# Last output tile and final norm of a three-layer block in parts of 384 and 128 tokens, not two of 256

## The reference, cut to what matters

```python
def rmsnorm_2(x, w):
    xf = x.astype(jnp.float32)
    y = xf * lax.rsqrt(jnp.mean(xf * xf, axis=-1, keepdims=True) + EPS)
    return (y * w.astype(jnp.float32)).astype(x.dtype)
...
        h = rmsnorm_2(x, norm_ffn_w[l])
        x = x + (jax.nn.silu(h @ w_gate[l]) * (h @ w_up[l])) @ w_down[l]
    return rmsnorm_2(x, final_norm_w)
```

## Time and profile before

| | us |
|---|---|
| median of 3 runs (2475.85, 2475.42, 2472.47) | 2475.42 |
| profiled execution, own time | 2472.24 |
| profiled execution, span of the trace | 2470.5 |
| PE busy (98% of the span) | 2432.2 |
| DVE busy (64%) | 1586.6 |
| ACT busy (43%) | 1064.8 |
| POOL busy (29%) | 723.8 |

### The profile page before, as it was taken

How to read it: one execution, slowest core, us unless ns; L and a number is a source line. 1 busy time by engine, 2 the same in 40 slices (tenths; PEclk the granted TensorE clock), 3 DMA queues, 4 the chain that set the end, 5 groups by cost and what they waited for, 6 DMA issues and landing times.

```text
span 2470.5 us, 30455 instructions
## 1 busy us (share of the span) xinstructions
PE 2432.2 (98%) x11856; PEld 1991.7 (81%) x11856; DVE 1586.6 (64%) x2021; ACT 1064.8 (43%) x1695; POOL 723.8 (29%) x426
## 2 busy tenths in 40 slices
PE   8999999999999999999999999999999988999998
PEld 6888888778888888888887778888887866888887
DVE  7887427667888317887137667887326655888712
ACT  5555114564555215554005564555213565555500
POOL 1001666522000560002665531001564422100164
PEclk9999999999999999999999999999999999999999
DMA  4332222103222223232222112422223111233222
GB/s 181 118 120 77 86 94 77 60 35 120 105 101 103 86 94 128 91 131 69 94 94 69 54 51 102 161 95 93 86 94 137 52 44 32 106 120 120 77 86 77
DMA packets 52382, 229.42 MB, mean 93 GB/s; under 512 B 7184, under 2 KB 10128, under 8 KB 39056
## 3 DMA queue, kind: packets, MB, share of 16 engines
q1 hardware_dynamic: 50528, 225.66, 26.1%
q10 hardware_dynamic: 1712, 1.82, 0.2%
HBM read 225.36 MB, written 2.10 MB: 92 GB/s over the span
## 4 chain that ended last, share of the span: by engine, by line
PE 95%; DVE 2%; ACT 1%; issue 1%; POOL 0%; DMA 0%; ACTq 0%; SPq 0%; DVEq 0%; POOLq 0%
PE bank L816 13%; PE bank L817 13%; PE bank L818 13%; PE bank L941 13%; PE bank L940 13%; PE bank L939 13%; PE bank L961 2%; PE bank L1048 2%; PE bank L1033 2%; PE bank L888 1%; PE bank L889 1%; PE bank L890 1%; PE bank L1017 1%; PE bank L1018 1%; PE bank L833 1%; PE bank L1270 1%
## 5 line engine op out<-in xcount | busy, mean ns | idle before, releaser
L770 POOL TENSOR_SCALAR wh<-raw 128x1024 fp32r<-128x1024 f32 x192 | 210.1, 1094 | 1698.0 <-PE bank L941 1082.2
L773 POOL TENSOR_TENSOR wl<-raw,wh 128x1024 fp32r<-128x1024 f32 x192 | 469.4, 2445 | 16.0
L816 PE MATMUL bank<-act_all,wh 128*128 128x512 f32 (+1 forms) x902 | 353.8, 392 | 0.0
L818 PE MATMUL bank<-act_all,wl 128*128 128x512 f32 (+1 forms) x902 | 346.7, 384 | 0.0
L817 PE MATMUL bank<-act_all,wh 128*128 128x512 f32 (+1 forms) x902 | 346.3, 384 | 0.0
L2044 DVE SCALAR_TENSOR_TENSOR x<-bank,x 128x512 f32<-128x512 f32 x63 | 43.2, 690 | 412.4 <-PE bank L818 412.4
L939 PE MATMUL bank<-wh,ss 128*128 128x512 f32 x540 | 211.3, 391 | 2.3 <-DVE plast L2130 2.3
L940 PE MATMUL bank<-wh,ss 128*128 128x512 f32 x540 | 210.9, 390 | 0.0
L941 PE MATMUL bank<-wl,ss 128*128 128x512 f32 x540 | 210.7, 390 | 0.0
L1534 ACT ACTIVATE wh<-rawa 128x1024 fp32r<-128x1024 f32 x135 | 143.3, 1062 | 155.9 <-PE bank L941 153.6
L2107 DVE TENSOR_TENSOR wl<-rawa,wh 128x1024 fp32r<-128x1024 f32 x135 | 165.2, 1223 | 62.3 <-ACT wh L1534 62.2
(11 more groups left out here) (374 smaller groups left out, 5208.8 us busy)
## 6 DMA issues: line engine op xcount, KB each, us to landing
raw<-in_stream SPq DMA_DIRECT2D x192, 512.0 KB, 3.3
rawa<-in_gu SPq DMA_DIRECT2D x60, 1024.0 KB, 4.8
raw<-in_gu SPq DMA_DIRECT2D x40, 1024.0 KB, 4.8
raw<-in_gu_small SPq DMA_DIRECT2D x20, 512.0 KB, 3.3
x<-in_x SPq DMA_DIRECT2D x8, 256.0 KB, 6.3
w1k<-in_w1k SPq DMA_DIRECT2D x1, 2048.0 KB, 7.9
w1v_low<-in_w1v SPq DMA_DIRECT2D x1, 1024.0 KB, 5.6
w1v_high<-in_w1v SPq DMA_DIRECT2D x1, 1024.0 KB, 7.6
```

The lines of the kernel that those rows point to most:

```text
L770: nc.gpsimd.tensor_scalar(wh[:, h % 2, :, :], src, 1.0, 1.0, ALU.mult, ALU.mult)\
L773: nc.gpsimd.tensor_tensor(wl[:, h % 2, :, :], src, wh[:, h % 2, :, :].bitcast(F32), ALU.subtract).then_inc(split_done, 1)
L816: mm = nc.tensor.matmul(bank, wh[:, slot, k, :], rh, start=start, stop=False)
L818: return nc.tensor.matmul(bank, wl[:, slot, k, :], rh, start=False, stop=stop)
```

## The change

The two parts of the last tile and of the norm are tokens 0 to 383 and 384 to 511 (`LAST_CUT = 3` of four groups of 128). POOL scales three tiles, not two, so DVE scales five. The sums of squares of tiles 0 to 6 are no longer made in bank 0 and added by DVE: `partial_sums` leaves them in banks 1 and 5 with `stop=False`, and `last_sums` adds the last tile's to them there; ACT takes the root straight from PSUM with the mean's factor as scale and `EPS` (set once at the start in `fin_part`) as bias. The blocks' order is new. On DVE, three of the first part's five scalings (tiles 5, 6, 7) move behind the second part's update and inverse, and the writes are grouped anew.

```diff
-LAST_POOL = 2
+LAST_POOL = 3
+LAST_CUT = 3
+LAST_TILES = (range(0, LAST_CUT), range(LAST_CUT, NQ))
+LAST_COLUMNS = (slice(0, LAST_CUT * P), slice(LAST_CUT * P, T))
...
-            for half, m, count in ((0, LAST_POOL, 6), (0, 0, LAST_POOL), (1, 2, 2), (1, 4, 2), (1, 6, 2)):
-                c = slice(2 * P * half, 2 * P * half + 2 * P)
+            for half, m, count in ((0, LAST_POOL, 2), (0, 5, 3), (0, 0, LAST_POOL), (1, LAST_POOL, 3), (1, 6, 2)):
+                c = LAST_COLUMNS[half]
...
-                    sp.wait_ge(fin_done, 6 * half + m + count - LAST_POOL)
+                    sp.wait_ge(fin_done, (KT - LAST_POOL) * half + m + count - LAST_POOL)
...
             def partial_sums():
...
-                for i in range(NQ):
-                    mm = nc.tensor.matmul(B[0][:, i:i + 1], rstd[:, i * P:(i + 1) * P], ones[:, 0:1], start=True, stop=True)
-                mm.then_inc(part_sums, 1)
+                for half in range(2):
+                    for i in LAST_TILES[half]:
+                        nc.tensor.matmul(B[(1, 5)[half]][:, i:i + 1], rstd[:, i * P:(i + 1) * P], ones[:, 0:1],
+                                         start=(i == LAST_TILES[half][0]), stop=False, skip_group_check=True)
 
             def last_sums(half):
                 pe.wait_ge(half_sq, half + 1)
-                for i in range(2 * half, 2 * half + 2):
+                for i in LAST_TILES[half]:
                     mm = nc.tensor.matmul(B[(1, 5)[half]][:, i:i + 1], sq[:, 3, i * P:(i + 1) * P], ones[:, 0:1],
-                                          start=True, stop=True)
+                                          start=False, stop=True, skip_group_check=True)
...
             for f in range(6, 14):
                 last_block(f, 0)
-            for f in range(6, 9):
-                last_block(f, 1)
             partial_sums()
             for f in range(14, FT):
                 last_block(f, 0)
-            for f in range(9, 12):
+            for f in range(6, 13):
                 last_block(f, 1)
             last_sums(0)
-            for f in range(12, 15):
+            for f in range(13, 18):
                 last_block(f, 1)
             last_rows(0)
-            for f in range(15, FT):
+            for f in range(18, FT):
                 last_block(f, 1)
             last_sums(1)
             last_rows(1)
...
-                act.wait_ge(fin_step, 4 * half + 3)
-                nc.scalar.activation(fin4[:, 2 * half:2 * half + 2], fin4[:, 2 * half:2 * half + 2], ACT.Sqrt).then_inc(fin_root, 1)
+                act.wait_ge(fin_set, 2)
+                act.wait_ge(half_sums, half + 1)
+                nc.scalar.activation(fin4[:, w], B[(1, 5)[half]][:, w], ACT.Sqrt, bias=fin_part[:, 0:1], scale=1.0 / D)\
+                    .then_inc(fin_root, 1)
...
+            V.memset(fin_part[:, :], EPS).then_inc(fin_set, 1)
...
+            def last_update(half, bank):
+                c = LAST_COLUMNS[half]
+                V.scalar_tensor_tensor(x[:, KT - 1, c], bank[:, c], 1.0, x[:, KT - 1, c], ALU.mult, ALU.add)\
                     .then_inc(fin_step, 1)
...
+            def last_scale(half, tiles):
+                c = LAST_COLUMNS[half]
                 dve.wait_ge(fin_rows, 2 * half + 1)
-                for m in range(LAST_POOL, KT):
+                for m in tiles:
                     V.scalar_tensor_tensor(x[:, m, c], x[:, m, c], gains2[:, 3, m:m + 1], B[LAST_ROWS[half][0]][:, c],
                                            ALU.mult, ALU.mult).then_inc(fin_done, 1)
+
+            dve.wait_ge(half_done, 1)
+            last_update(0, B[7])
+            last_inverse(0)
+            last_scale(0, range(LAST_POOL, 5))
+            dve.wait_ge(*last_done(KT - 1))
+            last_update(1, B[3])
+            last_scale(0, range(5, 6))
+            last_inverse(1)
+            last_scale(0, range(6, KT))
+            last_scale(1, range(LAST_POOL, KT))
```

More of the change, by code:

```diff
@@ L484, in build @@
         half_sq = sem("half_sq")
-        part_sums = sem("part_sums")
         fin_step = sem("fin_step")
@@ L1409, in _ @@
             last = DOWN_AT[4]
-            halves = ((B[7], slice(0, 2 * P)), (B[3], slice(2 * P, T)))
+            halves = ((B[7], LAST_COLUMNS[0]), (B[3], LAST_COLUMNS[1]))
             def last_block(f, half):
@@ L1425, in partial_sums @@
                 pe.wait_ge(sq_used, 9 * 8 + KT + 3)
-                for i in range(NQ):
-                    mm = nc.tensor.matmul(B[0][:, i:i + 1], rstd[:, i * P:(i + 1) * P], ones[:, 0:1], start=True, stop=True)
-                mm.then_inc(part_sums, 1)
+                for half in range(2):
+                    for i in LAST_TILES[half]:
+                        nc.tensor.matmul(B[(1, 5)[half]][:, i:i + 1], rstd[:, i * P:(i + 1) * P], ones[:, 0:1],
+                                         start=(i == LAST_TILES[half][0]), stop=False, skip_group_check=True)
             def last_sums(half):
                 pe.wait_ge(half_sq, half + 1)
-                for i in range(2 * half, 2 * half + 2):
+                for i in LAST_TILES[half]:
                     mm = nc.tensor.matmul(B[(1, 5)[half]][:, i:i + 1], sq[:, 3, i * P:(i + 1) * P], ones[:, 0:1],
-                                          start=True, stop=True)
+                                          start=False, stop=True, skip_group_check=True)
                 mm.then_inc(half_sums, 1)
             def last_rows(half):
-                pe.wait_ge(fin_step, 4 * half + 5)
+                pe.wait_ge(fin_step, 3 * half + 3)
                 for bank in LAST_ROWS[half]:
-                    for i in range(2 * half, 2 * half + 2):
+                    for i in LAST_TILES[half]:
                         tr = nc.tensor.transpose(B[bank][:, i * P:(i + 1) * P], cos[:, i * P:(i + 1) * P], ident[:, :])
@@ L1948, in _ @@
             for half in range(2):
-                c = slice(2 * P * half, 2 * P * half + 2 * P)
-                act.wait_ge(fin_step, 4 * half + 2)
+                c = LAST_COLUMNS[half]
+                w = slice(LAST_TILES[half][0], LAST_TILES[half][-1] + 1)
+                act.wait_ge(fin_step, 3 * half + 1)
                 nc.scalar.activation(sq[:, 3, c], x[:, KT - 1, c], ACT.Square).then_inc(half_sq, 1)
-                act.wait_ge(fin_step, 4 * half + 3)
-                nc.scalar.activation(fin4[:, 2 * half:2 * half + 2], fin4[:, 2 * half:2 * half + 2], ACT.Sqrt).then_inc(fin_root, 1)
+                act.wait_ge(fin_set, 2)
+                act.wait_ge(half_sums, half + 1)
+                nc.scalar.activation(fin4[:, w], B[(1, 5)[half]][:, w], ACT.Sqrt, bias=fin_part[:, 0:1], scale=1.0 / D)\
+                    .then_inc(fin_root, 1)
                 act.wait_ge(fin_rows, 2 * half + 2)
@@ L1956, in _ @@
             act.wait_ge(fin_pool, 2 * LAST_POOL)
-            act.dma_start(d["out"][:, 0:LAST_POOL, 2 * P:T], x[:, 0:LAST_POOL, 2 * P:T]).then_inc(out_done, 16)
+            act.dma_start(d["out"][:, 0:LAST_POOL, LAST_COLUMNS[1]], x[:, 0:LAST_POOL, LAST_COLUMNS[1]]).then_inc(out_done, 16)
         @block.vector
@@ L2789, in _, with last_inverse @@
                     .then_inc(fin_step, 1)
[L2790 to L2793, removed]
+            def last_inverse(half):
+                c, tiles = LAST_COLUMNS[half], LAST_TILES[half]
+                w = slice(tiles[0], tiles[-1] + 1)
                 dve.wait_ge(fin_root, half + 1)
@@ L2795, in _ @@
                 V.reciprocal(fin4[:, w], fin4[:, w]).then_inc(fin_step, 1)
-                dve.wait_ge(fin_step, 4 * half + 4)
-                V.tensor_copy(cos[:, c].rearrange("p (c n) -> p c n", c=2),
-                              fin4[:, w].rearrange("p (c a) -> p c a", a=1).to_broadcast([P, 2, P])).then_inc(fin_step, 1)
+                dve.wait_ge(fin_step, 3 * half + 2)
+                V.tensor_copy(cos[:, c].rearrange("p (c n) -> p c n", c=len(tiles)),
+                              fin4[:, w].rearrange("p (c a) -> p c a", a=1).to_broadcast([P, len(tiles), P]))\
+                    .then_inc(fin_step, 1)
```

## The result

| | before | after |
|---|---|---|
| median, 19 runs each | 2474.15 | 2478.43 |
| lowest and highest | 2471.93, 2475.85 | 2475.83, 2480.23 |
| ratio, with its 95% interval | | 1.0018 (1.0011 to 1.0025) |
| profiled execution, own time | 2472.24 | 2479.03 |
| its span | 2470.5 | 2477.2 |

What follows compares the result with a forecast made beforehand. PE bounds until its last block, then the first late write's issue and the bytes behind it. Issue +2.0 us and 0.65 MB more +1.95 make +3.9 on 2475.42: 2479.3 us, range 2473.4 to 2481.3.

Steps and rivals of the forecast that it cites:

- What bounds the kernel: End of the last tile: PE until its last matmul, then the first late write's issue and the bytes still to write.
- Price of a matmul by width: PE's last tile: 0.173 us at 384 columns, 0.1115 at 128, probably a weight-load floor; last block 3.1 us later.
- Rival A: PE's narrow matmuls cost half of those of 256 columns: 3.0 us fall away, +0.9, 2476.3 us; chance 0.12.
- Covers: Last unit's split and first part's update, square and spread finish before PE asks for them; no wait added.
- The second part's chain: Update to rows after PE's last block: 2.25 us, 0.85 less than before.
- spread copy 0.23: DVE's copy spreading the second part's inverse over 128 columns was taken to last 0.23 us.
- inside DVE's time: POOL's scalings, first part 2463.9 to 2466.8, second 2467.3 to 2468.6, were to end within DVE's own time.
- DVE's order and the first late issue: On DVE, tiles 6 and 7 stand behind the spread; SP's first late issue at 2467.45, 2.0 us later.
- Writes: After the first late issue 1.70 MB are left, before 1.05; at 330 GB/s 5.15 us, 1.95 more.
- Rival B: The writes do not bind; 3.45 us follow the last issue: +1.9, 2477.3 us; chance 0.06.
- Rival C: Second part's 512-byte output runs cost DMA as much as 1024-byte ones: +5.5, 2480.9 us, deciding from 2.6; chance 0.16.
- Rival D: The shorter tail after PE's last block wins; a gain over the bound would need 5 us of 9.2; chance 0.04.

Runs made afterwards that it cites:

- Run 1: Kernel after, but POOL's three first-part tiles are written before DVE's fifth scaling is waited for; median 2476.55 us against 2472.84 before, ratio 1.0014.
- run 5: Also e5_early: kernel after, with DVE's five first-part scalings ahead of the second part's update, first part's sums and rows earlier on PE; 2474.59 us, ratio 1.0004 to before.
- Run 4: Kernel after, with the second part's matmuls computing 256 columns, 128 of them unread; one profile, 32.0 us from last tile's first matmul to end, against 31.5.
- Run 2: Kernel after, with POOL starting on the first part only after the second part's spread; one profile, still 31.5 us from last tile's first matmul to end.
- e6_best: Kernel after, cut at 256, POOL two tiles, first part scaled before second's update, second part's DVE writes in 1, 1, 2, 2 tiles; 2472.09 us, ratio 0.9995 to before.
- e7_single: As e6_best, but every tile of the second part is written by itself, POOL's too; 2472.21 us against 2472.39 before, ratio 1.0000.
- e3_cut2: Kernel after, with the cut back at 256 and 256 tokens, all else kept; 2473.72 us, ratio 1.0003 to before.

## Why the prediction was right, point by point

Two of the points below rest on rows of before that were not shown so far, of PE and of DVE and POOL:

```profile
1931.37 0.63 PE L1198 MATMUL bank<-w2v,hid 128*31 128x64 f32 x8
...
2414.22 0.68 DVE L2024 TENSOR_TENSOR rstd<-rstd,sq 128x512 f32<-128x512 f32 x1
...
2443.43 2.40 POOL L773 TENSOR_TENSOR wl<-raw,wh 128x1024 fp32r<-128x1024 f32 x1
2444.14 2.24 DVE L2024 TENSOR_TENSOR rstd<-rstd,sq 128x512 f32<-128x512 f32 x1
```

- **What bounds the kernel.** Right, PE to its last block and then issue plus bytes. The sum "issue + 0.88 + bytes at 330 GB/s + 0.9" gave 6.93 from issue to end; the profile shows 6.89, as 0.9 to full DMA, 5.3 full and 0.7 to the end: two errors of 0.15 and 0.2 that cancel, by luck. Run 1, run 5 and the kernel after have issues at 23.51, 21.36 and 24.62, and the same 6.9 us behind each.
- **Price of a matmul by width.** Right: 0.11 and 0.17, and the last block at 21.03 for 21.02. Run 4 gives the reason by size: half the columns save 0.009 us. Which part of a matmul sets that floor no run varied, but two rows of before bear on it: eight matmuls of 64 columns that load 128 columns of weights each take 1.05 us (line 1210), and the eight of line 1198, which load 31 columns each, take 0.63, with starts about 0.06 apart and not 0.11. So the floor goes with the width of the weights, as the prediction supposed. The Trainium skill's 55.6 ns at 128 columns ("TensorE: Matmul & The Clock Gate", section "Wait — 56ns, not 53.3ns?") is not reached where weights change at each matmul, as here; an estimate of 107 ns for loading 128 columns, from columns / 1.2 in its section "LDWEIGHTS (loading the stationary operand)", agrees with the 0.11. Rival A falls.
- **Covers.** Right: no wait of PE is shown between the first and last block, and the split that PE needs ended at 2454.66, 1.2 before it.
- **The second part's chain.** Right up to the inverse, within 0.1 us. The step that was mis-sized is "spread copy 0.23": it took 0.66, since POOL was multiplying. Run 2 takes POOL away and finds 0.23; run 4 starts it 0.1 later against POOL, and it ends with POOL again (run 1 leaves the two as they were: 0.67). I had placed POOL's work "inside DVE's time" and charged nothing for the overlap. The trace of before had a price for such an overlap, which the prediction did not use: DVE's adding of squares (line 2024, both inputs in SBUF) takes 0.68 us while POOL is idle and 2.24 when it starts inside POOL's split, ending 0.55 after that (2446.38 after 2445.83). The Trainium skill, "GPSIMD Engine Reference", section "1. Specifications", says that POOL shares its interfaces to SBUF with VectorE and contends with its instructions that have two inputs in SBUF or run in a 2-port mode; these traces agree for the adding, and for the copy if it runs in such a mode, which no row shows, while the scaling at 2467.13 (one input in PSUM) takes 0.60 beside POOL and 0.61 without it in run 2.
- **DVE's order and the first late issue.** Right: two wide scalings and SP's wait for all five stand behind the spread, so its 0.43, and 0.07 from the steps ahead of it, passed straight into the issue: 24.62 for 24.12.
- **Writes.** Rival B falls: DMA is full without a gap. Rival C is right in its sign and not in its size: a run of 512 bytes takes 28.9 ns where one of 1024 took 48.6, so the second part's 1024 runs took 1.85 us on 16 engines, under the 2.6 at which C decides. The uniform 330 GB/s was wrong for both parts, by luck in opposite ways: those runs cost 0.26 more than by it, and the 768 late runs of 1536 bytes 0.26 less (3.31 for 3.57). The Trainium skill's 512 B as the least size for line rate ("DMA: Bandwidth & Descriptors", table at the top) doesn't hold in full here: the rate still rises beyond it, from about 286 GB/s to 361. Rival D falls; the shorter tail gives 0.6, not 5.

In sum: forecast 3.1 - 1.1 + 1.95 = +3.95 (the middle term is 4.21 less 24.12 - 21.02), shown 3.1 - 0.6 + 1.9 = +4.4.

## What to carry to other kernels

Cutting a stream of matmuls into a wide and a narrow part pays only while the narrow part costs by its columns: here 66 matmuls of 128 columns cost as much as 66 of 256 but for 0.6 us, so an uneven cut lengthened PE by 3.1 us, and no order tried with this cut gave that back in a tail of 9 us (best: 1.1 us over before). Where a kernel ends in writes, look for the last moment at which DMA is empty and count the bytes behind it: in these runs every wait that stood ahead of that issue went one to one into the end, and every early write that became a late one its own time on DMA, as long as DMA stayed full behind it (in run 2 it did not, and an earlier issue gained nothing). A short copy that is worked out from a quiet moment of DVE has to be priced again if POOL is busy on SBUF when it runs.

## What the runs showed of the hardware that was not expected

- A copy on DVE from SBUF to SBUF that starts inside a POOL multiplication ends 0.07 to 0.09 us after it (0.54 to 0.67 us long, 0.23 with POOL idle): it is held until POOL's instruction ends. The adding of squares in before is held in the same way (2.24 us for 0.68).
- The spread takes 0.23 us at 128 columns and 0.29 at 256, but 0.55 at 384 with POOL idle. The cause was not tried; it lies off the path.
- The granted clock in the tail falls to 0.5 (1.2 GHz) at different moments: under the rows in e6_best (four in 1.12 us, 0.51 granted), behind them in e7_single (0.66, 1.00 granted), with the same code on PE ahead of it and the same waits (0.96 us for the square, 0.94 for the spread). Why it fell earlier in the one is open.
- Writes of 512-byte runs move at about 286 GB/s with DMA full (289 in e5_early's last stretch), those of 1536 bytes at about 361, those of 1024 at 336 in e3_cut2. By single packets a run takes 28.9 ns at 512 bytes, 48.6 at 1024 and 69.0 at 1536: about 9 ns that do not go with the bytes, an estimate from these three.
- A matmul with its own weights costs 0.11 us from 1 to 128 columns where it loads 128 columns of weights, and about 0.06 at 64 columns where it loads 31 (line 1198).
